# A float32r trunk of two layers: the projections' matmuls read their moving columns from the last to the first

## The reference

```
for l in range(DEPTH):                                  # 2 layers
    h = rms_norm(x, pre_mix_norm[l])
    proj = h @ w_in[l]                                  # 2048 -> q, k, v, z, xbc, dt
    ... attention (8 heads x 128) and an SSD scan (16 heads x 64) ...
    h = concat(rms_norm(attn), rms_norm(y * silu(z))) @ w_out[l]     # 2048 -> 2048
    x = x + rms_norm(h, post_mix_norm[l])
    h = rms_norm(x, pre_mlp_norm[l])
    h = square(relu(h @ w_up[l])) @ w_down[l]           # 2048 -> 8192 -> 2048
    x = x + rms_norm(h, post_mlp_norm[l])
```

## Time and profile before

| | |
|---|---|
| time, median of the runs (2174.19 to 2174.86) | 2174.53 us |
| span of the profiled execution, first to last instruction | 2173.0 us |
| median less that span | 1.5 us |
| TensorE busy | 2160.4 us, 99% |
| VectorE busy | 1368.4 us, 63% |
| ScalarE busy | 1090.3 us, 50% |
| matmuls | 11445 |
| moved by DMA | 404.34 MB, 186 GB/s |

### The profile page before, as it was taken

One profiled execution on the slowest core, in us unless ns is written; L12 is line 12 of the kernel. 1 busy time (PEld: TensorE's weight loads), 2 busy tenths in 40 slices (PEclk: granted clock), 3 DMA queues, 4 the chain that ended last, 5 costly groups with the idle time before them and its releaser, 6 DMA issues.

```text
span 2173.0 us, 32439 instructions
## 1 busy us (share of the span) xinstructions
PE 2160.4 (99%) x11445; PEld 1856.4 (85%) x11445; DVE 1368.4 (63%) x1633; ACT 1090.3 (50%) x1658; POOL 109.0 (5%) x105
## 2 busy tenths in 40 slices
PE   9999999999999999999999999999999999999998
PEld 8888888888888888888898888888888888888887
DVE  7987564765555465456589975657555645554655
ACT  6554454653454454455465545546434534544543
POOL 2051000000000000000001410000000000000000
PEclk9999999999999999999999999999999999999999
DMA  7655555666665666665556555656666566656564
GB/s 225 180 154 174 155 192 186 198 190 198 191 193 193 192 189 196 192 193 193 179 154 194 156 165 155 197 180 193 205 194 193 181 205 177 208 193 192 177 208 149
DMA packets 232844, 404.34 MB, mean 186 GB/s; under 512 B 12508, under 2 KB 62452, under 8 KB 232244
## 3 DMA queue, kind: packets, MB, share of 16 engines
q1 hardware_dynamic: 231780, 398.57, 59.5%
q10 hardware_dynamic: 720, 4.26, 0.6%
q0 software_dynamic: 256, 0.33, 0.1%
HBM read 401.01 MB, written 2.10 MB: 186 GB/s over the span
## 4 chain that ended last, share of the span: by engine, by line
PE 98%; DMA 1%; issue 1%; DVE 0%; ACT 0%; POOL 0%; POOLq 0%; ACTq 0%; DVEq 0%
PE wide L1009 21%; PE wide L880 16%; PE wide L882 16%; PE wide L881 16%; PE wide L1017 11%; PE wide L956 8%; PE wide L963 4%; PE wide L1146 1%; DMA raw<-in_w_in 0%; PE wide L1048 0%; PE wide L931 0%; PE wide L933 0%; PE wide L934 0%; PE wide L1167 0%; PE wide L1187 0%
## 5 line engine op out<-in xcount | busy, mean ns | idle before, releaser
L1370 DVE TENSOR_TENSOR w_lo<-raw,w_hi 128x1024 fp32r<-128x1024 f32 x752 | 927.1, 1242 | 699.1 <-ACT w_hi L573 657.8
L573 ACT ACTIVATE w_hi<-raw 128x1024 fp32r<-128x1024 f32 x752 | 789.4, 1053 | 509.8 <-PE wide L882 451.3
L880 PE MATMUL wide<-w_hi,u_hi 128*128 128x512 f32 x1280 | 498.5, 389 | 0.0
L882 PE MATMUL wide<-w_hi,u_lo 128*128 128x512 f32 x1280 | 498.0, 389 | 0.0
L881 PE MATMUL wide<-w_lo,u_hi 128*128 128x512 f32 x1280 | 497.9, 389 | 0.0
L1009 PE MATMUL wide<-a_both,w_hi 128*128 128x512 f32 x1778 | 425.2, 389 | 0.0
L1009 PEld LDWEIGHTS wide<-a_both,w_hi 128*128 128x128 f32 x1778 | 333.6, 188 | 64.2
L882 PEld LDWEIGHTS wide<-w_hi,u_lo 128*128 128x128 f32 x1280 | 240.2, 188 | 50.2
L881 PEld LDWEIGHTS wide<-w_lo,u_hi 128*128 128x128 f32 x1280 | 240.3, 188 | 49.7
L880 PEld LDWEIGHTS wide<-w_hi,u_hi 128*128 128x128 f32 x1280 | 240.3, 188 | 49.4
L1017 PEld LDWEIGHTS wide<-a_both,w_lo 128*128 128x128 f32 x2032 | 250.2, 188 | 10.7
(11 more groups left out here) (255 smaller groups left out, 1545.8 us busy)
## 6 DMA issues: line engine op xcount, KB each, us to landing
raw<-in_w_up SPq DMA_DIRECT2D x256, 512.0 KB, 3.9
raw<-in_w_down SPq DMA_DIRECT2D x256, 512.0 KB, 4.5
raw<-in_w_in SPq DMA_DIRECT2D x176, 512.0 KB, 3.7
raw<-in_w_out SPq DMA_DIRECT2D x64, 512.0 KB, 4.4
zg<-in_post_mix_norm ACTq DMA_DIRECT2D x2, 1024.0 KB, 4.8
zg<-in_post_mlp_norm ACTq DMA_DIRECT2D x2, 1024.0 KB, 7.3
out<-x_sb SPq DMA_DIRECT2D x8, 256.0 KB, 2.5
x_sb<-in_x SPq DMA_DIRECT2D x3, 512.0 KB, 8.7
```

The costliest lines, as they stand in the source:

```text
L573: act.activation(w_hi[:, c % RING], raw[:, c % RING], ACT.Copy).then_inc(sem["hi_ready"], 1)
L880: pe.matmul(o, sh, wh, start=(k == 0 and not loaded), stop=False, skip_group_check=loaded)
L882: ins = pe.matmul(o, sl, wh, start=False, stop=(k == KT - 1), skip_group_check=loaded)
L1370: dve.tensor_tensor(lo[:, c % RING], raw[:, c % RING], hi[:, c % RING].bitcast(F32), ALU.subtract).then_inc(sem["split_done"], 1)
```

## The change

A helper turns the last dimension of an access pattern round: it starts at the last element and steps by -1. In `token_chunk`, `half_chunk` and `wide_chunk` it is put on the moving operand and on the output of each matmul, so that a column still lands where it landed. The stationary operand stays as it is. `feature_chunk`, the other branch of `wide_chunk`, the transposes and the products of attention and scan are unchanged.

```diff
+def backwards(a):
+
+    n = a.ap[-1][1]
+    return bass.AP(a.tensor, a.offset + n - 1, [*a.ap[:-1], [-1, n]])
...
             def token_chunk(c, banks, s_hi, s_lo, tiles=range(TT), loaded=False):
...
-                    wh, wl = (w[:, c % RING, kk * CB:(kk + 1) * CB] for w in (w_hi, w_lo))
-                    o = banks[t]
+                    wh, wl = (backwards(w[:, c % RING, kk * CB:(kk + 1) * CB]) for w in (w_hi, w_lo))
+                    o = backwards(banks[t])
...
-                            ins = pe.matmul(banks[m], wh, a_both[:, kt].rearrange("p a s -> p (a s)"),
+                            ins = pe.matmul(backwards(banks[m]), wh, backwards(a_both[:, kt].rearrange("p a s -> p (a s)")),
...
-                            ins = pe.matmul(banks[m][:, 0:SEQ], w(w_lo_off, kk, m), a_hi[:, c4 * 2 * CK + kk],
+                            ins = pe.matmul(backwards(banks[m][:, 0:SEQ]), w(w_lo_off, kk, m),
+                                            backwards(a_hi[:, c4 * 2 * CK + kk]),
...
-                            ins = pe.matmul(wide[j][:, m], wh, a_both[:, k].rearrange("p a s -> p (a s)"),
+                            ins = pe.matmul(backwards(wide[j][:, m]), wh,
+                                            backwards(a_both[:, k].rearrange("p a s -> p (a s)")),
...
-                            ins = pe.matmul(wide[j][:, m, 0:SEQ], w(w_lo_off, kk, m), a_hi[:, k], start=False, stop=False,
+                            ins = pe.matmul(backwards(wide[j][:, m, 0:SEQ]), w(w_lo_off, kk, m),
+                                            backwards(a_hi[:, k]), start=False, stop=False,
```

## The result

The changed kernel takes 2230.91 us (2230.80 to 2231.03) against 2174.53: 1.026 times as long, 95% interval 1.023 to 1.029. It is slower, by 56 us. Its profiled span is 2229.1 us, 56.1 over that of before.

A forecast was written before the change was run, and what follows sets the result against it. TensorE, busy 99% of the 2173.0 us span, was taken as the bound through its matmul start-to-start step. Changed matmuls 1999 us, untouched work 174 and 1.5 from span to median gave 2175 us; range 2050 to 2288 us.

The forecast's parts named there:

- (a): All changed matmuls: direction makes no difference to the rate; 2175 us, or 2192 with the 256-column matmuls disturbed; chance 0.54.
- rival (b): Weight load against moving stream in every changed matmul: disturbed state lasts also at 512 columns; 2218 to 2288 us; chance 0.16.
- 7408 steps at 512 and 2800 at 256 columns: Count of changed matmuls in `token_chunk`, `wide_chunk` and `half_chunk`; at 226.8 and 113.8 ns, 1999 us, 92% of the span.
- dearer variant of (a): 256-column matmuls alone disturbed, at 120 instead of 113.8 ns a step: 17 us more, 2192 us.
- I take neither: Backward read in changed matmuls: rejects both a gain of 119 us and half rate, 430 ns for 512 columns.
- come back to 227 in a few matmuls: 512-column steps after a disturbance: eight averaged 231.3 ns, a later group was clean; used against a lasting disturbed state.
- the shift is undone: Weight loads beside the stream: a descending start could cancel the 16-element shift of `w_lo`; 17 us for 256-column matmuls alone.
- Rival (c): Every changed matmul loses pairing of neighbouring columns on read or write, half rate: 3963 us; chance 0.15.
- Rival (d): Changed matmuls: the lost cycle belongs to ascending order and disappears, 119 us less, 2056 us; half of it, 2115; chance 0.13.
- the cycle lost in 17: TensorE's moving stream: 0.443 ns a column against 0.417 at 2.4 GHz; 13.4 ns at 512 columns, 7.1 at 256.
- R: Theory of the experiments, not the prediction: a backward-read stream has its own slower rate, whatever runs beside it; 233 ns expected.

The follow-up runs named there:

- read_only: Changed kernel with the helper taken from the outputs, so only the moving operand is read backwards: 2231.18 us, 1.026 times the kernel before.
- within_back: Changed kernel with groups of 16 elements in ascending order, each reversed inside, on moving operand and output: 2520.93 us, 1.159 times the kernel before.
- shift_fwd: Kernel before, all reads forwards, with both rooms of weights 16 elements (64 bytes) further for every block: 2198.85 us, ratio 1.011.
- shift_bwd: Changed kernel with both rooms of weights 16 elements (64 bytes) further for every block: 2229.86 us, 1.025 times the kernel before.
- half_load_bwd: Changed kernel with the low-weight product of `token_chunk` taking 64 of its 128 stationary columns: 2231.64 us, 1.026 times the kernel before.
- small_load_bwd: Changed kernel with 32 stationary columns in three quarters of `token_chunk` and all low-weight products of `wide_chunk`: 2231.58 us, 1.026 times the kernel before.

## Why the prediction was right or wrong

The forecast (a) did not come: 2175 was said, 2231 measured. The range, 2050 to 2288, holds it because rival (b) had been taken in. With 238 us from end to end and a cause for (b) that the runs don't bear out, that is in part luck.

- The bound was read rightly. TensorE sets the end, nothing else moved, and the account of 7408 steps at 512 and 2800 at 256 columns gives the result once the rate is known. The 256-column steps were put 17 us up in the dearer variant of (a); they took 12.
- The step that failed is "I take neither" under **Reading backwards**: from equal bytes and an equal footprint I took an equal rate, and so put the read's term at nothing. `read_only` shows that direction alone costs 6.6 ns in 226.7. The Trainium skill (SBUF — State Buffer, "SBUF: two separate sides") would have four reads to each 16-byte line at full rate in either direction; here 233.3 against 226.7 ns, and 266.8 in `within_back`, differ. The measurement decides.
- The second failure is the sentence that those steps "come back to 227 in a few matmuls". That was seen of forward streams and carried over to a backward one, which doesn't come back: 233 in each stretch shown.
- Rival (b) had the size: 2218 to 2288, with 231 to 236 ns given as its mark. Of its mechanism half holds. Forward streams do depend on addresses (`shift_fwd`: 233.1 ns in L1017, 113.8 in place of 120 in `feature_chunk`). But "the shift is undone" fell with `shift_bwd`, and that the meeting with weight loads makes the backward cost was not borne out by `half_load_bwd` and `small_load_bwd`. Its number was right with a cause that the runs don't support.
- Rival (c), half rate for lost pairs, did not occur on the read or the write. Rival (d), that the cycle lost in 17 belongs to ascending order, did not occur either; with smaller loads the forward stream didn't fall below 226.7 ns on average, in `token_chunk` or in the up projection, so that loss doesn't come from the load's size.

What stays open: the backward stream kept its rate with loads of 128, 64 and 32 columns, but no kernel ran a backward stream with no load beside it, so that R holds without any load is argued, not shown. The loads themselves lasted 188 ns in the kernel before and in the changed one, and 191 to 192 ns in `within_back`. Why steps back of 32 elements cost and those of 128 don't was not taken further, nor what in `within_back` costs 40 ns. No version tried is faster than the kernel before. The 113.8 ns of `feature_chunk` in `shift_fwd` would be worth 336 x 6.2 ns = 2 us if it could be had there alone, within what a comparison here can resolve; it was not tried alone.

## What to carry to other kernels

Where the chain is TensorE throughout and its waits are a few microseconds, read the start-to-start step of the matmuls: any change of an access pattern is a change of that step, times the count. Equal bytes and an equal footprint don't make an equal step: the order of the moving read counts, that of the output's write did not at a step of -1. A forward float32r stream may sit in a favourable state that another address or, as in `token_chunk` here, a smaller weight load spoils, so measure such an edit even where it takes work away.

## What the runs showed of the hardware that was not expected

- Fewer weights to load made the forward kernel slower: 64 columns in one product of three of `token_chunk`, 2188.5 us; 32 columns in three quarters of `token_chunk` and in the low products of the up projection, 2193.2; 128 in all, 2174.7. The steps that grew are those of `token_chunk`.
- A plain reversal costs 2.6%, a reversal inside 64-byte groups 15.9%, a reversal of 128-element groups nothing within 0.1%.
- With the stationary tile 64 bytes further (and the tensors behind it possibly 512), the step of a forward stream that reads the same values in the same order went from 227 to 233.1 ns at 512 columns (L1017) and from 120 to 113.8 ns at 256 (`feature_chunk`).
